# Delta rule's inputs: keys' layer from the first tile on, the next layer's input in a second buffer, small products spread over the steps

## What is computed

```python
dx = jnp.pad(h, ((0, 0), (1, 0), (0, 0)))[:, :-1] - h        # h: normed input
x_rkv = h[:, :, None, :] + dx[:, :, None, :] * mu[:3]
rkv = jnp.einsum('bsnd,nde->bsne', x_rkv, w_in)              # three 1024 x 1024 layers
xw, xa, xg = h + dx * mu[3], h + dx * mu[4], h + dx * mu[5]
zw = w0 + jnp.tanh(xw @ w1) @ w2
decay = jnp.exp(-jnp.exp(-jax.nn.softplus(-zw) - 0.5))
a = jax.nn.sigmoid(a0 + (xa @ a1) @ a2)
g = jax.nn.sigmoid(xg @ g1) @ g2
kk = heads(k * k_k); kk = kk / jnp.maximum(jnp.sqrt(jnp.sum(kk * kk, -1, keepdims=True)), 1e-12)
k = k * (1.0 + (a - 1.0) * k_a)
y = wkv7_scan(rh, heads(decay), kh, vh, -kk, kk * ah)        # the scan over the tokens
```

## Time and profile before

| | us |
|---|---|
| median of 3 runs | 2424.54 (2422.43 to 2425.61) |
| the profiled execution, its own time | 2422.46 |
| its span in the profile | 2420.4 |
| stage 4's last matmul starts | 765.78 |
| layer r's first matmul starts | 816.88 |
| layer v's end (ScalarE's next `round` starts) | 911.37 |

### The profile page before, as it was taken

One profiled execution on the slowest core, in us unless ns is written; L12 is line 12 of the kernel. 1 busy time (PEld: TensorE's weight loads), 2 busy tenths in 40 slices (PEclk: granted clock), 3 DMA queues, 4 the chain that ended last, 5 costly groups with the idle time before them and its releaser, 6 DMA issues.

```text
span 2420.4 us, 32778 instructions
## 1 busy us (share of the span) xinstructions
PE 2283.6 (94%) x12883; PEld 1850.6 (76%) x12883; DVE 1495.0 (62%) x2061; ACT 1158.3 (48%) x1677; POOL 176.5 (7%) x287
## 2 busy tenths in 40 slices
PE   8999999999997978789999999998999899969998
PEld 6888778887886666668887888866888788848886
DVE  6656757647655676656657656655665765647655
ACT  5445545446444443245445444444544544545444
POOL 1001000001001010310001000001000100041000
PEclk9999999999998989989999999999999999989999
DMA  7556636555655330046555555512655555606552
GB/s 246 184 191 221 214 109 223 186 174 183 200 187 188 112 131 3 3 143 210 170 189 197 178 189 197 184 53 85 201 180 181 183 185 182 199 20 193 186 183 104
DMA packets 289894, 396.19 MB, mean 164 GB/s; under 512 B 11688, under 2 KB 193264, under 8 KB 289744
## 3 DMA queue, kind: packets, MB, share of 16 engines
q1 hardware_dynamic: 284800, 377.33, 47.1%
q0 software_dynamic: 4800, 16.72, 2.1%
q10 hardware_dynamic: 144, 0.07, 0.0%
HBM read 393.03 MB, written 1.05 MB: 163 GB/s over the span
## 4 chain that ended last, share of the span: by engine, by line
PE 74%; DVE 7%; ACT 3%; issue 2%; DMA 2%; POOL 1%; DVEq 0%; SPq 0%; POOLq 0%; ACTq 0%
PE bank L485 21%; PE bank L487 21%; PE bank L486 21%; PE bank L511 1%; PE bank L1301 1%; PE bank L499 1%; DVE wl L779 1%; ACT wh L600 1%; ACT JUNK L607 1%; PE bank L1704 1%; DMA raw<-in_a_w_out_dram 1%; PE bank L1721 1%; DVE TMP L817 1%; DVE qPS L1658 0%; DVE H L837 0%
## 5 line engine op out<-in xcount | busy, mean ns | idle before, releaser
L779 DVE TENSOR_TENSOR wl<-raw,wh 128x1024 fp32r<-128x1024 f32 x708 | 859.0, 1223 | 592.2 <-ACT wh L600 591.8
L600 ACT ACTIVATE wh<-raw 128x1024 fp32r<-128x1024 f32 x708 | 744.0, 1058 | 670.5 <-PE bank L487 642.3
L485 PE MATMUL bank<-wh,XH 128*128 128x512 f32 x2032 | 812.9, 400 | 20.0 <-DVE XL L796 6.1
L486 PE MATMUL bank<-wl,XH 128*128 128x512 f32 x2032 | 796.5, 392 | 0.0
L487 PE MATMUL bank<-wh,XL 128*128 128x512 f32 x2032 | 796.1, 392 | 0.0
L485 PEld LDWEIGHTS bank<-wh,XH 128*128 128x128 f32 x2032 | 384.8, 189 | 106.0 <-ACT wh L600 8.8
L487 PEld LDWEIGHTS bank<-wh,XL 128*128 128x128 f32 x2032 | 384.3, 189 | 83.3
L486 PEld LDWEIGHTS bank<-wl,XH 128*128 128x128 f32 x2032 | 385.0, 189 | 75.8 <-issue 0.5
L485 PE MATMUL bank<-wh,AH 128*128 128x512 f32 x704 | 276.0, 392 | 0.0
L487 PE MATMUL bank<-wh,AL 128*128 128x512 f32 x704 | 274.1, 389 | 0.0
L486 PE MATMUL bank<-wl,AH 128*128 128x512 f32 x704 | 274.0, 389 | 0.0
(11 more groups left out here) (307 smaller groups left out, 1729.9 us busy)
## 6 DMA issues: line engine op xcount, KB each, us to landing
raw<-in_ffn_w_dram SPq DMA_DIRECT2D x184, 512.0 KB, 4.7
raw<-in_ffn_wi_dram SPq DMA_DIRECT2D x176, 512.0 KB, 4.6
raw<-in_ffn_w_dram SPq DMA_DIRECT2D x40, 1024.0 KB, 4.8
raw<-in_ffn_wo_dram SPq DMA_DIRECT2D x40, 1024.0 KB, 4.9
raw<-in_a_wqkv_dram SPq DMA_DIRECT2D x18, 1024.0 KB, 4.8
raw<-in_a_w_in_dram SPq DMA_DIRECT2D x16, 1024.0 KB, 5.2
raw<-in_b_w_in_dram SPq DMA_DIRECT2D x12, 1024.0 KB, 4.9
bc<-in_norm_g_dram POOLq DMA_DIRECT2D x16, 512.0 KB, 5.6
```

Source lines behind the costliest of these rows:

```text
L485: pe.e.matmul(o, a, h, start=(k == 0), stop=False)
L486: pe.e.matmul(o, a, l, start=False, stop=False)
L600: act.e.activation(self.wh[j % N_W][:, 0:p.size], self.raw[p.chunk % N_RAW][:, p.at:p.at + p.size], ACT.Copy).then_inc(*self.rounded.up(j))
L779: dve.e.tensor_tensor(self.wl[j % N_W][:, 0:p.size], self.raw[p.chunk % N_RAW][:, p.at:p.at + p.size], self.wh[j % N_W][:, 0:p.size].bitca ...
```

## The change

- The layers run in the order k, r, v, and k has `head=6`, so it begins with 12 steps of tile 0. Tile 0 is squared on ScalarE ahead of tile 1's last square of stage 4, normed on ScalarE, transposed, and mixed half a tile (q = 0, 1: four of the eight k) at a time; four `leave`s of stage 4's end move behind this. Tile 1 is transposed before steps 6 and 7.
- r reads from a second pair of buffers (XH2, XL2), mixed while k runs; v's input is mixed while r runs.
- The first product of LoRA g goes beside steps 18 to 25 of k, those of a and w beside steps 8 to 15 of r (each half of one bank); the second products of a and w before steps 17, 21, 25, 29 of r, g's before steps 5, 9, 13, 17 of v; the decay's before 21 and 25, scl before 29. All use banks 6 and 7.
- Mixed inputs of g and w are made on GpSimd (eight operations of 1024 columns), the one of a on VectorE. The sigmoids' scale and shift go from VectorE to ScalarE.
- Weights of the LoRAs lie in other places; the last 32 rows of g's second weight (g2b) go where a's bias was, by a DMA that waits for that bias's last use.

The diff, cut to its core (removed functions stand in the listing above):

```diff
-            for m in range(3):
-                add(n, "rkv"[m], DK, cut(rows(A["b_w_in"][0, m]), range(2)))
+            for m, name in ((1, "k"), (0, "r"), (2, "v")):
...
+                    self.act_square_h(act, n + 1, 0)
                 self.act_square_out(act, n, 1, ss)
...
+            return
         for p in layer.parts[max(first, half):-1] if self.goes_on(n) else layer.parts[max(first, half):]:
...
+                self.rsqrt(pool, self.cols(T, "hss")[:, t:t + 1], 1.0 / D, RMS_EPS, "h", t)
     def pool_start(self, pool):
...
+        rwkv = self.layers[5, "k"].parts[0].chunk
         scan = self.layers[5, "out"].parts[0].chunk
         for c in range(self.all_chunks):
+            if c == scan:
+                self.sp_rwkv_rk(sp)
+            if c == scan + 2:
+                self.sp_rwkv_g2(sp)
             if c == scan + 4:
                 self.sp_rwkv_scan(sp)
                 sp.wait_ge(self.moved, "yo", 1, 1)
             self.load(sp, c)
-            if c == rwkv + 5:
+            if c == rwkv + 3:
                 self.sp_rwkv_in(sp)
...
+    def pe_turn_h(self, pe, t, q):
+        bank = self.turn_bank(pe, ("h", t, q), (self.made, "ht", t, q))
+        pe.wait_ge(self.moved, "hn", t)
+        for i in range(4):
+            k = 4 * q + i
+            m = pe.e.transpose(bank[:, i * P:(i + 1) * P], self.hn[:, t, k * P:(k + 1) * P], self.ident[:, :])
+        m.then_inc(*self.turned.up("h", t, q))
+    def pe_beside_k(self, pe, step):
+        if step in (6, 7):
+            self.pe_turn_h(pe, 1, step - 6)
+        if 18 <= step < 26:
+            k = step - 18
+            if k == 0:
+                for part in range(2):
+                    self.take_bank(pe, 6 + part, (self.moved, "th", "g"))
+                pe.wait_ge(self.d_one["g1"])
+            pe.wait_ge(self.figured, "mix", 0, k // 4)
+            for part, c0, c1 in ((0, 0, P), (1, P, 160)):
+                m = pe.e.matmul(self.bank(6 + part)[0:c1 - c0, 0:S], self.W1[0][:, k, c0:c1], self.LO[0][:, k, :],
+                                start=(k == 0), stop=(k == DK - 1))
+            if k == DK - 1:
+                m.then_inc(*self.product.up("lora", "g"))
+    def pe_beside_r(self, pe, step):
+        if 8 <= step < 16:
+            k = step - 8
+            if k == 0:
+                self.take_bank(pe, 6, (self.moved, "th", "w"))
+                pe.wait_ge(self.d_one["a1"])
+                pe.wait_ge(self.d_one["w1"])
+            pe.wait_ge(self.made, "mix", k)
+            pe.wait_ge(self.figured, "mix", 2, k // 4)
+            for part in (1, 0):
+                m = pe.e.matmul(self.bank(6)[self.HALF[part], 0:S], self.W1[1 + part][:, k, :], self.LO[1 - (part == 0)][:, k, :],
+                                start=(k == 0), stop=(k == DK - 1))
+            if k == DK - 1:
+                m.then_inc(*self.product.up("lora", "aw"))
+        if step in (17, 21, 25, 29):
+            b, t = divmod((step - 17) // 4, 2)
+            pe.wait_ge(self.moved, "th", "w")
+            pe.wait_ge(self.d_one["a2"])
+            pe.wait_ge(self.d_one["w2"])
+            for part, which in enumerate("aw"):
+                h = self.HALF[part]
+                bank = self.take_bank(pe, 6 + part, (self.made, "sig", which, b, t))
+                pe.e.matmul(bank, self.TH[h, 2, t * P:(t + 1) * P], self.W2[h, b * 512:(b + 1) * 512], start=True,
+                            stop=True).then_inc(*self.product.up("lora2", which, b, t))
+    def pe_beside_v(self, pe, step):
+        if step in (5, 9, 13, 17):
+            b, t = divmod((step - 5) // 4, 2)
+            pe.wait_ge(self.d_one["g2"])
+            pe.wait_ge(self.d_one["g2b"])
+            bank = self.take_bank(pe, 6 + t, (self.moved, "g", b, t))
+            c, at = slice(b * 512, (b + 1) * 512), slice(t * P, (t + 1) * P)
+            pe.e.matmul(bank, self.TH[:, 0, at], self.G2[:, c], start=True, stop=False)
+            pe.e.matmul(bank, self.TH[0:32, 1, at], self.bct[0][0:32, c], start=False, stop=True).then_inc(
+                *self.product.up("lora2", "g", b, t))
+        if step in (21, 25):
+            self.pe_decay(pe, 0, (step - 21) // 4, (6, 7))
+        if step == 29:
+            bank = self.take_bank(pe, 6, (self.moved, "scl"))
+            for t in range(T):
+                for p in range(8):
+                    m = pe.e.matmul(bank[:, 3 * p + t:3 * p + t + 2], self.LW[:, t, p * P:(p + 1) * P],
+                                    self.CU[:, 2 * P + 2 * t:2 * P + 2 * t + 2], start=(t == 0 and p == 0),
+                                    stop=(t == 1 and p == 7), skip_group_check=True)
+            m.then_inc(*self.product.up("scl"))
+        pe.wait_ge(self.moved, "lw")
...
+    def act_square_h(self, act, n, t):
+        act.wait_ge(self.resid, n - 1, t, 1)
+        self.square(act, self.H[:, t, :], self.cols(T, "hss")[:, t:t + 1], "h", t)
+    def act_normed(self, act, t):
+        act.wait_ge(self.rs, "h", t)
+        act.e.activation(self.hn[:, t, :], self.H[:, t, :], ACT.Copy, scale=self.cols(T, "hss")[:, t:t + 1]).then_inc(
+            *self.moved.up("hn", t))
...
+        self.act_normed(act, 0)
+        self.act_square_h(act, n, 1)
+        self.act_mixed(act, 1, 0, 0)
+        self.act_normed(act, 1)
+        self.act_mixed(act, 1, 0, 1)
+        for name, to in (("k", self.K), ("r", self.R), ("v", self.VV)):
...
+    def act_beside_k(self, act, i):
+        if i == 0:
+            for q in range(2):
+                self.act_mixed(act, 1, 1, q)
+        if 2 <= i < 6:
...
+        if i == 7:
+            th = self.TH
+            act.wait_ge(self.product, "lora", "g")
+            act.wait_ge(self.made, "xm", 0, 1, 1)
+            act.e.activation(th[:, 0, 0:S], self.bank(6)[:, 0:S], ACT.Tanh, scale=0.5)
+            act.e.activation(th[0:32, 1, 0:S], self.bank(7)[0:32, 0:S], ACT.Tanh, scale=0.5).then_inc(
+                *self.moved.up("th", "tanh"))
+            act.wait_ge(self.moved, "th", "tanh")
+            act.e.activation(th[:, 0, 0:S], th[:, 0, 0:S], ACT.Copy, scale=0.5, bias=0.5)
+            act.e.activation(th[0:32, 1, 0:S], th[0:32, 1, 0:S], ACT.Copy, scale=0.5, bias=0.5).then_inc(
+                *self.moved.up("th", "g"))
...
+    def act_beside_r(self, act, i):
+        th = self.TH
+        if i < 4:
+            if i == 0:
+                act.wait_ge(self.used[1], self.layers[5, "k"].end[1])
+            self.act_mixed(act, 2, *divmod(i, 2))
+        if i == 3:
+            act.wait_ge(self.product, "lora", "aw")
+            act.e.activation(th[0:64, 2, 0:S], self.bank(6)[0:64, 0:S], ACT.Copy)
+            act.e.activation(th[64:128, 2, 0:S], self.bank(6)[64:128, 0:S], ACT.Tanh).then_inc(*self.moved.up("th", "w"))
+        if i in (4, 5):
+            t = i - 4
+            act.wait_ge(self.made, "kk", t)
+            act.e.activation(self.TB[:, t, :], self.KK[:, t, :], ACT.Square).then_inc(*self.moved.up("kk2", t))
+        if i >= 5:
+            self.act_rates(act, *divmod(i - 5, 2))
...
+    def act_rates(self, act, b, t):
+        for which, to in (("a", self.AA), ("w", self.LW)):
+            x = to[:, t, b * 512:(b + 1) * 512]
+            act.wait_ge(self.made, "sig", which, b, t)
+            act.e.activation(x, x, ACT.Tanh, scale=0.5).then_inc(*self.moved.up("sig", which, b, t))
+        for which, to, f in (("a", self.AA, 0.5), ("w", self.LW, -0.5 * EXP_HALF)):
+            x = to[:, t, b * 512:(b + 1) * 512]
+            act.wait_ge(self.moved, "sig", which, b, t)
+            act.e.activation(x, x, ACT.Copy, scale=f, bias=f).then_inc(
+                *self.moved.up("aa" if which == "a" else "lw", *(() if (b, t) == (1, 1) else (b, t))))
+    def act_beside_v(self, act, i):
+        if i == 0:
+            self.act_rates(act, 1, 1)
+        if 2 <= i < 6:
+            b, t = divmod(i - 2, 2)
+            act.wait_ge(self.product, "lora2", "g", b, t)
+            act.e.activation(self.GG[:, t, b * 512:(b + 1) * 512], self.bank(6 + t), ACT.Copy).then_inc(
+                *self.moved.up("g", b, t))
+        if i in (6, 7):
+            self.act_decay(act, 0, i - 6, [self.att[i][:, :] for i in range(3)])
+        if i == 7:
...
+        dve.wait_ge(self.turned, "h", t, q)
+        dve.e.tensor_tensor(HT[:, k, at:at + P], self.bank(self.place["turn", ("h", t, q)]).rearrange("p (k s) -> p k s", k=4),
+                            g, ALU.mult).then_inc(*self.made.up("ht", t, q))
+        dve.wait_ge(self.made, "ht", t, q)
+        if t == 0:
+            dve.wait_ge(self.resid, n - 1, 1, 1)
+            dve.e.tensor_scalar(DX[:, k, 0:1], HT[:, k, 0:1], -1.0, None, ALU.mult).then_inc(*self.made.up("dx0", q))
+        first = max(at, 1)
+        dve.e.tensor_tensor(DX[:, k, first:at + P], HT[:, k, first - 1:at + P - 1], HT[:, k, first:at + P],
+                            ALU.subtract).then_inc(*self.made.up("dx", t, q))
...
+        for j in range(4):
+            k = 4 * q + j
```

(133 more changed lines are left out.)

322 lines of the change are left out of this document (100 added, 222 removed).

## The result

The changed kernel takes 2445.86 us (median of 4 runs, 2440.15 to 2447.31) against 2425.07 (4 runs, 2422.43 to 2427.04): ratio 1.0082, 95% interval 1.0063 to 1.0101. It is slower, as the likeliest case said, but by 20.8 us where 6.1 were forecast, and 4.9 us above the upper end of the range.

A forecast was written before the change was run, and what follows sets the result against it. TensorE, busy 94% of the span, was taken as the bound. For the three layers, 775.4 + 104.9 work + 30.2 waits + 6.8 clock = 917.3 against 911.2, 6.1 us later: 2430.5 us, range 2415 to 2441.

The forecast's parts named there:

- the likeliest case: Whole kernel: v ends at 917.3 against 911.2, 6.1 us later, told as 2430.5 us; chance 0.42.
- k's first matmul, 775.4: Start of k: tile 0's norm, transposes and mixes let k's first matmul start at 775.4, where r's was at 816.88.
- PE's work, 104.9: TensorE's work from 775.4 on: 96 steps at 0.683 (65.6), LoRA and decay products, scl, tile 1's transposes; together 104.9 us.
- the bounds: Ranges for single terms; first products of a and w may overlap in different halves of a bank, up to -3.6 us.
- Waits of r and v: TensorE waits on late bank readers or g2b's DMA: r 2.1 and 9.0, v 3.4, 1.0, 4.0, 2.8 us.
- k, step 11: 7.9: In k, TensorE waits 7.9 us for VectorE's late `leave` of part 5, 3.5 us of work times 2.3 for POOL contention.
- the bound of 12: Upper bound in us of k's wait at step 11, with POOL slowed as well and `leave` 7 late.
- Clock: 6.8: Half clock for about four steps after the first gap (2.2), after k's 7.9 (2.2) and behind scl (2.4): 6.8 us.
- Three places: Where the clock was to fall: after the first gap, after k's wait at step 11, and behind scl.
- The clock falls in every wait: Rival: six waits of 2.8 us or more in r and v; five falls of 2.2 give +11, 2441; chance 0.13.
- contention at the start was not mild: Rival claimed no contention on VectorE after tile 1's DX in k: -8.7 us, 2421.8; chance 0.27.
- the products don't fit in the order written: Rival claimed the products do fit between steps, r's and v's waits shrinking to nothing: 20.2 us less, 2410; chance 0.13.

The follow-up runs named there:

- the last kernel: Kernel with readers earlier, mixes on VectorE and the later edits (0.9863), plus 13 unread products ahead of tile 0's transposes and 16 behind: 2393.55 us, ratio 0.9856.
- A: Changed kernel with POOL's mixes in operations of 256 columns (1.0065) or 2048 (1.0109), started later (1.0073), or moved to VectorE (1.0043).

## Why the prediction was wrong

By its own steps:
- *k's first matmul, 775.4.* It came at 778.26 with stage 4 ending 2.55 later, so 775.7. Right.
- *PE's work, 104.9.* In the last kernel from k's first product to the scan's first transpose are 109.9 us, of them 2.5 waits and at most 3.4 for the half clock behind scl: 104.0. The sum is right, by luck in part, for its terms were off both ways: the first products of a and w ran side by side (both halves of a bank start within 0.01 us of each other; the bounds had this) and took some 4.7 us for 7.3, their second products 4.6 for 6.8, but the 96 steps some 70 for 65.6, as the step behind a slipped product is longer.
- *Waits of r and v.* Step 17: 1.1 for 2.1; 21 to 29: 10.2 for 9.0; v: 2.8, 0.8, 4.2, 2.7 for 3.4, 1.0, 4.0, 2.8. Right in size, and by the reason given: moving the reader one part took those of steps 21 to 29 and of v away. The wait at step 17 went when VectorE made v's mixes ahead, which fits its own reason.
- *k, step 11: 7.9.* 13.0. **This step failed**: "Times 2.3 this is 8.0". Contention was priced as a ratio on VectorE's durations, from two operations of 512 columns. What the runs show is that a small operation of VectorE ends only with POOL's running instruction, whatever its own size: the four mixes took 6.57 us for some 2.5, the two low halves 3.43 for 2.8, the `leave` 2.91 for 2.8. 13.0 also lies above the bound of 12. +5.1; the sum of all waits +4.6.
- *Clock: 6.8.* **The larger failure.** From k's first product to v's end went 161.2 us in the changed kernel; less 34.8 of waits and 104.0 of work, 22.4 are left and put down to the clock; eight falls at the 2.6 measured in r would be 21. "Three places" were eight: behind k's start, behind k's long wait, and behind six waits of r and v (the last is the one behind scl, which the forecast had). The rival "The clock falls in every wait" held: the five new falls of r and v came, at 2.6 to 2.8 us each in place of 2.2. The reason against it, that those waits are much shorter than 11.78 us, was weak: the trace of before, outside the stretch that the prediction read, has short waits with a fall behind them. TensorE there, with the idle time ahead in brackets:
```profile
1889.22 1.09 PE L499 MATMUL bank<-ident,H 128*128 128x128 f32 x4 [4.47 <-DVE H L837]
```
The four us from there have a granted clock of 0.50; behind waits of 1.97 (1064.26) and 2.48 us (1286.00) it is 0.57. What decides for shorter waits stays open: the clock held behind 1.6 us ahead of k and of v in the kernel before and fell behind 1.4 and 1.7 in kernels of the experiments.
- The other rivals: contention at the start was not mild (A), and the products don't fit in the order written; they do once the readers stand one part earlier.

Forecast +6.1, measured +25.7 (939.45 - 768.56 = 170.9 against 145.2): +4.6 waits, +15.6 clock, +0.3 start, -0.9 work, 19.6 together. The 4 us won in the scan were not in the forecast ("the scan starts from v's end as before"), and they hide as much of the miss. The rival and the forecast were given as cases that exclude each other, and both happened. That 2430.5 + 11 for the falls + 4.6 for the waits is 2446, as measured, is luck: the falls cost 15.6 more and not 11, and the scan gave 4.0 back.

## What to carry to other kernels

- A wait costs its length and the clock behind it. Where a change turns one long gap of TensorE into many short ones, count the falls: here eight took some 22 us, more than any one of the waits. That the same total of idle time is cheapest in one piece follows from this, but no run tried it.
- When products are slipped between the steps of a stream, look at where the *reader* of their bank stands in the other engines' programs: it must come before the work that waits for the same step, or each product waits for a part of the stream.
- Before work goes to POOL beside VectorE, count VectorE's small operations there: each can last as long as one whole instruction of POOL. Short pieces halved TensorE's wait (13.0 to 6.2); no work on POOL there did better (3.9).

## What the runs showed of the hardware that was not expected

- VectorE's operations with two SBUF operands and POOL's alternate: beside POOL's instructions of 256, 1024 and 2048 columns, four mixes of 128 columns took 2.21, 6.57 and 12.14 us, 1.14 alone.
- Waits of TensorE of 2.8 to 4.2 us, and with the earlier readers even one of 1.4, were followed by 3 to 7 us at 1.2 GHz; waits of 1.6 and 1.1 were not, and one of 2.36 us was in one execution and not in the other. The clock also fell with no wait at all: behind the 16 scl products of 2 columns (32 records, 4.25 us), with TensorE busy throughout (885 to 890 us, 0.56, above).
- Twelve useless products of 512 columns (2.88 us) in a wait of 3.1 to 4.0 us left no time lost and won 2.6 us each time; 30 of them (6.97 us) in a wait of 3.6 won nothing.
